# A fifth small expert in the grouped stage of a two-layer decoder trunk, and three small moves at its ends

## The reference, cut to what matters

```
logits = xt @ w_router                       # 256 tokens, 8 experts
top_logits, top_idx = lax.top_k(logits, 2)   # two experts for each token
gates = jax.nn.softmax(top_logits, axis=-1)
# for each expert e and the rows x routed to it:
y = (jax.nn.silu(x @ w1[e]) * (x @ w3[e])) @ w2[e]    # 1024 -> 3584 -> 1024
out[token] += gate * y
# then x = x + gate_f * rms_norm(y, norm_ffn_post)
```

## Time and profile before

| | us |
|---|---|
| median of 3 runs (1725.46 to 1734.82) | 1733.24 |
| the profiled execution | 1733.83 |
| its span in the profile | 1731.2 |
| PE busy | 1641.7 (95%) |
| DVE busy | 1449.8 (84%) |
| ACT busy | 1049.7 (61%) |
| expert 0 | about 717 to 849 |
| grouped stage | 848.8 to 1469.2 |
| two loop jobs | 1469.2 to 1713.8 |
| last norm and store | 1713.8 to 1731.2 |

### The profile page before, as it was taken

The page is one execution under the profiler, slowest core; times in us unless marked ns, Lnnn a source line. Parts: engine busy times, 40 slices in busy tenths (PEclk is TensorE's granted clock), DMA queues, the critical chain, the costliest instruction groups (busy, mean ns, idle before and its releaser), DMA issues.

```text
span 1731.2 us, 23943 instructions
## 1 busy us (share of the span) xinstructions
PE 1641.7 (95%) x8645; PEld 1347.3 (78%) x8645; DVE 1449.8 (84%) x1830; ACT 1049.7 (61%) x1303; POOL 58.0 (3%) x84
## 2 busy tenths in 40 slices
PE   5998988999999889999989999999999999999996
PEld 5987868999988878788867677777777766888875
DVE  4787777788878774799789999989998998988887
ACT  1554433433455443576676867777877787767774
POOL 0000000000010000100000000000000000010110
PEclk9898999999999899899999999999999999999998
DMA  9456555889835655698899999999999999999994
GB/s 308 142 171 195 195 170 165 284 281 293 267 122 171 195 182 171 220 390 320 310 352 341 377 332 361 367 352 359 378 367 344 378 393 365 353 385 367 364 390 165
DMA packets 270308, 503.71 MB, mean 291 GB/s; under 512 B 12646, under 2 KB 113272, under 8 KB 270200
## 3 DMA queue, kind: packets, MB, share of 16 engines
q1 hardware_dynamic: 262736, 489.72, 79.8%
q0 software_dynamic: 3072, 11.01, 1.8%
q10 hardware_dynamic: 4392, 1.57, 0.4%
HBM read 492.84 MB, written 9.44 MB: 290 GB/s over the span
## 4 chain that ended last, share of the span: by engine, by line
issue 43%; PE 39%; DVE 11%; POOL 1%; ACT 1%; DVEq 1%; ACTq 1%; POOLq 1%; DMA 1%; SPq 0%
PE ps L1925 9%; PE ps L1927 9%; PE ps L1926 9%; DVE lo_ring L1825 8%; PE ps L2254 5%; PE ps L2253 4%; DVEq L1838 1%; PE ps L2217 1%; POOL rstd L845 1%; ACT stage_hi L1188 1%; DMA weight_ring<-in_moe_w_dram 1%; DVE m_silu L1830 0%; DVE a_lo L1856 0%; PE ps L2255 0%; DVE m_act L1852 0%
## 5 line engine op out<-in xcount | busy, mean ns | idle before, releaser
L1825 DVE TENSOR_TENSOR lo_ring<-weight_ring,stage_hi 128x1024 fp32r<-128x1024 f32 x420 | 486.7, 1218 | 37.1 <-ACT stage_hi L1188 33.9
L1188 ACT CAST stage_hi<-weight_ring 128x1024 fp32r<-128x1024 f32 x420 | 414.5, 1050 | 31.6 <-DMA weight_ring<-in_moe_w_dram 30.7
L1568 DVE TENSOR_TENSOR lo_ring<-weight_ring,stage_hi 128x1024 fp32r<-128x1024 f32 x252 | 291.7, 1217 | 18.2 <-ACT stage_hi L1117 17.6
L1117 ACT CAST stage_hi<-weight_ring 128x1024 fp32r<-128x1024 f32 x252 | 246.8, 1053 | 40.9 <-DMA weight_ring<-in_moe_w_dram 38.6
L1317 DVE TENSOR_TENSOR lo_ring<-weight_ring,stage_hi 128x2048 fp32r<-128x2048 f32 x81 | 184.9, 2291 | 74.0 <-ACT stage_hi L981 66.8
L1925 PE MATMUL ps<-h_hi,stage_hi 128*128 128x256 f32 x800 | 235.9, 295 | 9.0 <-DVE h_lo L1280 7.2
L1926 PE MATMUL ps<-h_lo,stage_hi 128*128 128x256 f32 x800 | 231.8, 290 | 0.0
L1927 PE MATMUL ps<-h_hi,lo_ring 128*128 128x256 f32 x800 | 231.3, 289 | 0.0
L981 ACT CAST stage_hi<-weight_ring 128x2048 fp32r<-128x2048 f32 x81 | 153.5, 1905 | 122.0 <-DMA weight_ring<-in_w_in_dram 62.5
L1925 PE MATMUL ps<-stage_hi,xe_hi 128*128 128x512 f32 x448 | 181.7, 406 | 4.6 <-DVE lo_ring L1568 2.4
L1926 PE MATMUL ps<-lo_ring,xe_hi 128*128 128x512 f32 x448 | 176.2, 393 | 0.0
(11 more groups left out here) (383 smaller groups left out, 2616.0 us busy)
## 6 DMA issues: line engine op xcount, KB each, us to landing
weight_ring<-in_moe_w_dram SPq DMA_DIRECT2D x336, 1024.0 KB, 7.6
weight_ring<-in_w_mod_dram SPq DMA_DIRECT2D x48, 1024.0 KB, 5.5
weight_ring<-in_w_in_dram SPq DMA_DIRECT2D x36, 1024.0 KB, 5.5
weight_ring<-in_ffn_w_dram SPq DMA_DIRECT2D x33, 1024.0 KB, 7.0
weight_ring<-in_w_out_dram SPq DMA_DIRECT2D x12, 1024.0 KB, 5.0
moe_rows<-y_moe POOLq DMA_DIRECT2D x6, 512.0 KB, 5.2
moe_rows<-y_e POOLq DMA_DIRECT2D x3, 512.0 KB, 7.8
x_tok<-in_x_dram SPq DMA_DIRECT2D x1, 1024.0 KB, 10.7
```

Of the source, the lines that this page charges most:

```text
L1117: nc.scalar.copy(jst_hi[i % JSTAGES][:, part], ring[:, n % RING, part]).then_inc(hi_ready, 1)
L1188: nc.scalar.copy(jst_hi[g % JSTAGES][:, part], ring[:, n % RING, part]).then_inc(hi_ready, 1)
L1568: nc.vector.tensor_tensor(ring_lo[:, n % RING, part], ring[:, n % RING, part], raw(jst_hi[i % JSTAGES][:, part]), ALU.subtract).then_inc(l ...
L1825: nc.vector.tensor_tensor(ring_lo[:, n % RING, part], ring[:, n % RING, part], raw(jst_hi[g % JSTAGES][:, part]), ALU.subtract).then_inc(l ...
```

## The change

`NSMALL` goes from 4 to 5: the expert of rank 2 leaves the loop and becomes a fifth small one in the grouped stage, which now has 252 slots instead of 210. The loop is left with one job. `EXTRA` (places for jobs that do not fit) goes from 4 to 5, and POOL clears one more block of 128 rows and one more of 64 rows of the table. A temporary table of DVE, `epick`, now lies in another one. The narrow loads are issued by ACT after its first cast of a weight slot and not before the layers, with semaphores of their own. At the end the copy of `selT` moves from DVE to ACT, the square of the last norm writes to `y_back` and not to `xn`, so that DVE's product with the gate no longer waits for it, and DVE's operations on the two blocks of tokens are interleaved.

```diff
-EXTRA = 4
+EXTRA = 5
-COL_RANK = [NE - 1, 0, 0, 3, 4, 5, 6, 1, 2]
-COL_BIG, COL_SMALL, COL_LOOP = 1, 3, 7
+COL_RANK = [NE - 1, 0, 0, 2, 3, 4, 5, 6, 1]
+COL_BIG, COL_SMALL, COL_LOOP = 1, 3, 8
-NSMALL = 4
+NSMALL = 5
@@ group()
-        behind = [3, 1 if ch == 0 else 3, 6, 6, 3, 3] if ch < NCH - 1 else [6, 6, 6, 6, 2, 0]
+        behind = [4, 2 if ch == 0 else 4, 7, 7, 4, 4] if ch < NCH - 1 else [7, 7, 7, 7, 4, 0]
-PLACES_C = 22
+PLACES_C = 29
@@ build()
-        epick = m("epick", [P, NCOL, NE])
+        epick = pick[:, 1]
@@ block.scalar
-            for l in range(DEPTH):
-                act.dma_start(wdt[:, l], k_rows(w_in[l], 0, KT, OFF["dt"], SH)).then_inc(par_landed, 16)
-            act.dma_start(wrt[:], k_rows(moe_router[0], 0, KT, 0, NE)).then_inc(par_landed, 16)
+            def narrow_loads():
+                for l in range(DEPTH):
+                    act.dma_start(wdt[:, l], k_rows(w_in[l], 0, KT, OFF["dt"], SH)).then_inc(wdt_landed[l], 16)
+                act.dma_start(wrt[:], k_rows(moe_router[0], 0, KT, 0, NE)).then_inc(wrt_landed, 16)
@@ at the end of a split (the cast of a slot)
+                    if n_split == 1:
+                        narrow_loads()
@@ the end, block.scalar
+            act.wait_ge(sT_done, 1)
+            nc.scalar.copy(selT[:].rearrange("p t n -> p (t n)"), ps[:, IDXB, 0:TT * P]).then_inc(sT_ready, 1)
             for t in range(TT):
                 act.wait_ge(ysub_done, t + 1)
-                square_block(DEPTH - 1, "post_ffn", t, y_moe[:, t, :])
+                square_block(DEPTH - 1, "post_ffn", t, y_moe[:, t, :], y_back[:, :, 0, :])
@@ the end, block.vector
-            dve.wait_ge(sT_done, 1)
-            nc.vector.tensor_copy(selT[:].rearrange("p t n -> p (t n)"), ps[:, IDXB, 0:TT * P]).then_inc(sT_ready, 1)
-            for t in range(TT):
+            def to_tokens(t):
                 dve.wait_ge(back_done, t + 1)
                 nc.vector.tensor_tensor(y_moe[:, t, :], pair(2 * t), y_moe[:, t, :], ALU.add)
                 nc.vector.drain().then_inc(ysub_done, 1)
-                if t == 0:
-                    dve.wait_ge(grow_ready, 2 * DEPTH)
-                dve.wait_ge(xs_ready, block_of(DEPTH - 1, "post_ffn", t))
-                gated(t, y_moe[:, t, :], gate_last)
-            for t in range(TT):
-                added(DEPTH - 1, "post_ffn", t)
+            to_tokens(0)
+            dve.wait_ge(grow_ready, 2 * DEPTH)
+            gated(0, y_moe[:, 0, :], gate_last)
+            to_tokens(1)
+            added(DEPTH - 1, "post_ffn", 0)
+            gated(1, y_moe[:, 1, :], gate_last)
+            added(DEPTH - 1, "post_ffn", 1)
@@ block.tensor
-                    pe.wait_ge(par_landed, 17 * 16)
+                    pe.wait_ge(par_landed, 14 * 16)
@@ the step "dt"
+                    pe.wait_ge(wdt_landed[l], 16)
@@ ahead of the router
+            pe.wait_ge(wrt_landed, 16)
```

More of the change, by code:

```diff
@@ L632, in build @@
         par_landed = sem("par_landed")
+        wdt_landed = [sem("wdt_landed%d" % l) for l in range(DEPTH)]
+        wrt_landed = sem("wrt_landed")
         consts = sem("consts")
@@ L952, in squares, with square_block @@
                 nc.scalar.drain().then_inc(ss_ready, 1)
-            def square_block(l, name, t, a):
-                nc.scalar.activation(xn[:, t, :], a, ACT.Square, accum_out=sumsq[:, rq(l, name), t:t + 1])
+            def square_block(l, name, t, a, squared=xn):
+                nc.scalar.activation(squared[:, t, :], a, ACT.Square, accum_out=sumsq[:, rq(l, name), t:t + 1])
                 nc.scalar.drain().then_inc(xs_ready, 1)
@@ L1680, in more_jobs @@
                 nc.vector.drain()
-                nc.vector.tensor_tensor(epick[:], ohk[:], iota[:, 0:NE].unsqueeze(1).to_broadcast([P, NCOL, NE]), ALU.mult)
+                nc.vector.tensor_tensor(epick, ohk[:], iota[:, 0:NE].unsqueeze(1).to_broadcast([P, NCOL, NE]), ALU.mult)
                 nc.vector.tensor_tensor(pick[:, 0, new], ohk[:, new], cap[:].unsqueeze(1).to_broadcast([P, EXTRA, NE]), ALU.mult)
@@ L1725, in back_rows @@
             def back_rows():
-                nc.vector.tensor_scalar(step1[:], place[:], 1.0, 6.0 * P, ALU.is_ge, ALU.mult)
-                nc.vector.tensor_scalar(step_few[:], place[:], 3.0, -6.0 * P, ALU.is_ge, ALU.mult)
-                nc.vector.tensor_scalar(step7[:], place[:], 7.0, -7.0 * P, ALU.is_ge, ALU.mult)
+                nc.vector.tensor_scalar(step1[:], place[:], 1.0, 7.0 * P, ALU.is_ge, ALU.mult)
+                nc.vector.tensor_scalar(step_few[:], place[:], 2.0, -6.0 * P, ALU.is_ge, ALU.mult)
+                nc.vector.tensor_scalar(step7[:], place[:], 7.0, -8.0 * P, ALU.is_ge, ALU.mult)
                 nc.vector.scalar_tensor_tensor(out=base[:], in0=place[:], scalar=float(P), in1=base[:],
```

## The result

The changed kernel takes 1739.64 us (median of 12 runs), the kernel before 1732.15 in the same comparison: a ratio of 1.0038, 95% interval 1.0020 to 1.0056. The prediction was 1712. It is slower by a little, and by no more than about the 0.5% taken for no change. One of its 12 runs took 1973.55 us at a granted clock of 0.749; ratios and intervals here leave such slow runs out. The profiled execution took 1739.71 us (span 1738.0), against 1733.83 (1731.2) before.

A forecast was written before the change was run, and what follows sets the result against it. DVE was taken to set every chunk of the grouped stage, with PE close and transfers 3 to 4% behind. Terms -121.5 + 103 - 1.5 - 1.8 = -21.8 took 1733.83 to 1712 us, range 1698 to 1731.

The forecast's parts named there:

- The bound: Grouped stage: DVE, busy 684 us, sets every chunk; PE needs at most 696, transfers 666.
- The loop, -121.5: Loop: one job fewer, with no extra job appearing, saves 121.5 us.
- The grouped stage, +103: Grouped stage: 42 more slots lengthen it by 103 us, bounds 84 and 124.
- sum by units: Grouped stage: the larger of the engines' needs in each unit gives 97.8 us a chunk; above 738 us refutes it.
- 1.5 us of loss: Grouped stage: engines taking turns in being late cost 1.5 us a chunk, 11 us of the growth.
- parts of the gather and the fold (3 us): Grouped stage: gather and fold add 3 us to the 89 us of growth in seven chunks.
- mean slot: Grouped stage: each of 252 slots still costs 2.955 us, 744.6 in all; total 1733, chance 0.14.
- The start, -1.5: Start: moving the narrow loads takes 1.5 us off, bounds 0 and 2.5.
- The rival with 8 us: Start: ACT's issue of the narrow loads or wdt's arrival lies open, 8 us instead of -1.5; total 1720, chance 0.06.
- The end, -1.8: End: moving selT's copy and dropping DVE's waits for the square save 1.8 us, bounds -1.2 and -3.0.
- The fifth expert fits: Loop: rank 2 has 43 rows of 64; otherwise one more job of 121.5 us, total 1833, chance 0.04.
- The 24 us for the loss: Grouped stage: engines hindering each other cost an estimated 24 us against PE's 696, which gives 720.

The follow-up runs named there:

- the aligned order: The changed kernel with its slots reordered so that each small chunk begins and ends at a big slot: 1718.26 us, ratio to the kernel before 0.9912.

## Why the prediction was wrong

*The bound:* DVE's busy time came to within 1 us of the forecast. That DVE sets the chunk is shown for the aligned order, where taking work from DVE, after little had come of taking it from PE, moved the stage to the next bound. In the changed order nobody took work off DVE.

*The loop, -121.5:* right; one job less, and -119.8 from the group's end to the start of DVE's copy of the last y_e.

*The grouped stage, +103:* wrong, it was +127.5, and at 748 us the stage is above the 738 that the prediction named as refuting its sum by units. Yet "Taking the larger each time, a chunk is 4 x 13.65 + 2 x 21.6 = 97.8 us", with 1.5 us of loss, was nearly right: 99.3 was forecast and 100.46 measured where there is no gather. That is 1.2 us a chunk, some 8 in seven; which engine's wait they come from stays open. The step that failed is the next one, "To this come parts of the gather and the fold (3 us)", with "89 us in seven chunks": one chunk without a gather was taken seven times, and gathers, folds and the end of the group were priced as work, not by where they stand. Beyond seven regular chunks (7 x 15.3 = 107.2 us of growth) the changed order grew by 20.3 us, the aligned one by 3.0, just what was forecast. These 17 us are the order's: 9.0 in the last chunk, of which the run with another end gets back 6.8 in its last two units, and 8.4 in the chunks with a gather. In the four units with a gather alone the changed order spends 5.7, 6.8, 3.5 and 2.0 us more than in their like, 18.0 in all, against 13.4 in the aligned order; the rest of the 8.4 comes in the units beside them. I had the two orders before me and read only how many slots stand in a unit. What passes the wait on at a gather is shown in rows for one of the four.

*The rival "mean slot" (1733):* its number for the stage, 744.6, was near, and its total nearer to 1739.64 than mine, by luck: its mechanism was not there. With half the bytes the stage was as long, and another order of the same slots made it 17.4 us shorter. What spoke for it, transfers busy for 98%, was no evidence.

*The start, -1.5:* wrong and small. The share of the narrow packets in a stretch was not a delay of the chain; the cover on ACT held, and nothing was gained. The rival with 8 us did not come (by its own terms it stood at 1721.5, not 1720).

*The end, -1.8:* the mechanism held, 2.7 us in the trace, and the timing cannot tell either from nothing.

*The fifth expert fits:* right, no extra job.

The chances were the larger mistake. The 24 us for the loss were an estimate taken from an order in which everything fitted, and the upper bound for the stage's growth, 124 us, was that of another mechanism. Had I asked what the order's misfit could cost, a result without gain would have had more than 0.14.

## What to carry to other kernels

When work of one period is interleaved with work of another, count not only what stands in each unit but where the rare steps stand, those at the change from one piece of work to the next and those at the very end: what follows them must be covered by independent work of the engine that waits. Measure them apart from the regular stretch, since one regular chunk taken seven times leaves them out. Changing the number of experts from four to five asked for a new order (six small slots behind most big ones), not for one more slot in each unit; that alone is worth 1.2% here. And a resource busy for 98% is shown to be a bound only when less work for it makes the stage shorter.

## What the runs showed of the hardware

- Waits of PE of 3.5 and 4.1 us in the middle of full work brought the clock from 2.4 to 1.2 GHz, and the 13 matmuls behind the second took 5.7 us instead of 3.0. So did 3.68 us of narrow matmuls (64 columns, the gather) with a wait of 1.45 us behind them: 0.52 in the next 3.5 us. In the aligned orders the longest waits were 1.6 and 2.0 us, and the granted clock stayed at 1.00. So such a wait costs more than its length.
- The busy share of the transfer engines did not tell whether they were the bound: 0.97 at 359 GB/s and 0.59 at 185, with the same length of the stage, and 1.03 at 389 when they were.
- The same three narrow loads took ACT 6.8 us to issue right behind its other loads, and 4.7 us when it had issued none for 27 us.
